# Two queues for the weights of a two-layer streaming encoder: bf16 loads on SyncE, casts paced by matmuls, activation sums moved in the down stage

## The reference

```
layer 0: x += conv_mixers(rmsnorm(x))      # in-projection 1024 -> 2560, two causal convolutions, out-projection
         x += swiglu(rmsnorm(x))           # (silu(h @ Wg) * (h @ Wu)) @ Wd, hidden width 2816
layer 1: x += attention and spatial gating # in-projection 1024 -> 2560, band of 576 keys, out-projection
         x += swiglu(rmsnorm(x))           # other weights
```

## Time and profile before

| | us |
|---|---|
| median of 3 runs | 2945.32 |
| profiled execution | 2949.8 |
| its span (core 0, the slowest) | 2948.3 |
| span of the fastest core | 2926.0 |
| TensorE (PE) busy on core 0 | 2734.8 |
| DVE busy | 1906.9 |
| ACT busy | 1344.7 |
| POOL busy | 472.7 |

### The profile page before, as it was taken

How to read it: one execution, slowest core, us unless ns; L and a number is a source line. 1 busy time by engine, 2 the same in 40 slices (tenths; PEclk the granted TensorE clock), 3 DMA queues, 4 the chain that set the end, 5 groups by cost and what they waited for, 6 DMA issues and landing times.

```text
span 2948.3 us, 49213 instructions; the slowest of 8 cores (2926.0 to 2948.3 us)
## 1 busy us (share of the span) xinstructions
PE 2734.8 (93%) x19840; PEld 1786.7 (61%) x19840; DVE 1906.9 (65%) x3375; ACT 1344.7 (46%) x2538; POOL 472.7 (16%) x946
## 2 busy tenths in 40 slices
PE   6789999767999995999989899999899999999999
PEld 3445555445777773667744555555567777776776
DVE  7667777644555572666757677777665555766655
ACT  2222222133444442555545676677644444454444
POOL 3112211120000011110132344443400000100000
PEclk9889999888999997999999999999999999999999
DMA  9697665796423479784682344445542322534332
GB/s 191 164 177 166 176 171 131 162 142 109 123 78 87 135 193 127 163 190 118 171 166 60 84 111 109 111 114 151 175 138 86 123 78 87 185 129 140 87 129 101
DMA packets 325592, 393.42 MB, mean 133 GB/s; under 512 B 221298, under 2 KB 221826, under 8 KB 325236
## 3 DMA queue, kind: packets, MB, share of 16 engines
q1 hardware_dynamic: 282836, 308.44, 37.6%
q0 software_dynamic: 42528, 81.84, 16.6%
HBM read 255.16 MB, written 167.48 MB: 143 GB/s over the span
## 4 chain that ended last, share of the span: by engine, by line
PE 82%; DMA 6%; DVE 4%; ACT 3%; SPq 3%; POOL 1%; issue 1%; POOLq 0%; DVEq 0%; ACTq 0%
PE ps L687 79%; SPq L717 3%; DMA hT<-h 2%; PE ps L971 2%; DMA xr<-xp 1%; ACT tr L639 1%; DVE xr L650 1%; DMA WiA<-wie 1%; ACT hr L639 1%; DMA WDB<-wdb 1%; PE ps L697 1%; DMA WoC<-woo 1%; DVE hr L654 0%; PE ps L708 0%; POOL E L650 0%
## 5 line engine op out<-in xcount | busy, mean ns | idle before, releaser
L639 ACT ACTIVATE ps<-ps 128x512 f32<-128x512 f32 x720 | 419.6, 583 | 458.8 <-PE ps L687 430.2
L650 DVE TENSOR_TENSOR xr<-ps,xr 128x512 f32<-128x512 f32 (+1 forms) x404 | 272.3, 688 | 162.8 <-PE ps L687 116.0
L687 PE MATMUL ps<-hT,WiA 128*128 128x512 bf16 x1280 | 287.2, 383 | 1.2 <-ACT hT L639 1.1
L639 ACT ACTIVATE hr<-xr 128x1024 bf16<-128x1024 f32 x132 | 138.9, 1052 | 260.3 <-DVE xr L650 196.6
L654 DVE SCALAR_TENSOR_TENSOR hr<-xr,rsr,gain 128x1024 bf16<-128x1024 f32 x132 | 169.2, 1282 | 82.9 <-POOL rsr L650 82.5
L687 PEld LDWEIGHTS ps<-hT,WiA 128*128 128x128 bf16 x1280 | 124.7, 99 | 149.3 <-issue 6.4
L687 PE MATMUL ps<-hT,WGC 128*128 128x256 bf16 x1536 | 187.2, 274 | 9.2 <-DMA WGC<-wgb 5.3
L687 PE MATMUL ps<-hT,WGB 128*128 128x256 bf16 x1280 | 157.5, 275 | 39.3 <-DVE xr L650 33.0
L687 PE MATMUL ps<-hT,WGA 128*128 128x256 bf16 x1536 | 188.0, 275 | 5.8 <-DMA hT<-h 3.7
L687 PE MATMUL ps<-hT,WiC 128*128 128x512 bf16 x768 | 180.4, 379 | 0.7 <-DVE tr L1435 0.4
L687 PEld LDWEIGHTS ps<-hT,WGC 128*128 128x128 bf16 x1536 | 145.2, 98 | 35.3 <-DMA WGC<-wgb 5.9
(11 more groups left out here) (321 smaller groups left out, 5263.4 us busy)
## 6 DMA issues: line engine op xcount, KB each, us to landing
x<-xr SPq DMA_DIRECT2D x160, 512.0 KB, 3.7
xr<-x SPq DMA_DIRECT2D x160, 512.0 KB, 5.7
xr<-xp SPq DMA_DIRECT2D x64, 512.0 KB, 5.8
h<-hr SPq DMA_DIRECT2D x124, 256.0 KB, 3.1
wgb<-wgu POOLq DMA_DIRECT2D x76, 256.0 KB, 14.9
yp<-xr SPq DMA_DIRECT2D x32, 512.0 KB, 3.1
wdb<-wd POOLq DMA_DIRECT2D x44, 256.0 KB, 11.7
WGC<-wgb POOLq DMA_DIRECT2D x12, 512.0 KB, 6.7
```

What stands on the lines that cost most here:

```text
L639: return tag(e.activation(out=R(out), in_=R(in_), func=func, **kw))
L650: return P.add(eng, lambda e, tag: tag(e.tensor_tensor(out=R(out), in0=R(a), in1=R(b), op=op)), [a, b], [out], c)
L687: ins = e.matmul(R(out), l, r, start=st, stop=sp_, skip_group_check=True)
```

## The change

1. Loads from bf16 scratch go to SP's queue, in a stream "wl" of depth 10. Casts stay on POOL's queue in the stream "w", whose depth goes from 6 to 24.
2. `background` takes the place of `cast_some`. Each cast gets a dependence on the matmul that was recorded last before it, so that POOL waits for PE's semaphore (m_pe) ahead of it. The casts are recorded in the hooks behind single gate/up products (in stage A behind its steps), 5 per tile of pass A, 7 of pass B, 5 of stage C, and none behind the last product of a tile.
3. `hsums` gets a dependence on `P.mid`, the matmul that ends the first part of the down stage's second half. `tsums` get a lower priority.
4. The planner's rates change (SP 150 to 230 GB/s, POOL 250 to 200, SP latency 4.0 to 2.5 us), a rule adds a `prime` matmul where no free PSUM bank has been written in full (5 in the program where there were 2), and the down weights of a pass are recorded in its first tile, behind that tile's transposes.

```diff
-        P.depths = {"w": 6, "xl": 6, "xst": 6, "hst": 4, "htr": 4, "ms": 4, "mg": 2, "out": 4}
+        P.depths = {"w": 24, "wl": 10, "xl": 6, "xst": 6, "hst": 4, "htr": 4, "ms": 4, "mg": 2, "out": 4}
-        rate = {"sp": 150e3, "pool": 250e3}
+        rate = {"sp": 230e3, "pool": 200e3}
...
-                op = dma("pool", dst[:, c:c + step], src[:, c:c + step], "w", list(rd), [dst[:, c:c + step]],
-                         step * 128 * (2 if bf else 4))
+                op = dma("sp" if bf else "pool", dst[:, c:c + step], src[:, c:c + step], "wl" if bf else "w", list(rd),
+                         [dst[:, c:c + step]], step * 128 * (2 if bf else 4))
...
-                tt("dve", f(d), f(a), f(b), ALU.subtract, fast=True)
+                tt("dve", f(d), f(a), f(b), ALU.subtract, fast=True, boost=-60)
...
-        def cast_some(ly, p, n):
-            for key in casts[ly, p][:n]:
...
+        def background(n=1):
+            for key in back[:n]:
+                pace = [P.last["pe"]]
...
+                for d in pace:
+                    op.deps.setdefault(d, False)
+            del back[:n]
...
+        def hsums(layer, p, after=None):
+            n0 = len(P.ops)
+            hsums_(layer, p)
+            if after is not None:
+                for op in P.ops[n0:]:
+                    op.deps.setdefault(after, False)
...
             prod(b11, u, 2, (1, 0), order, False)
+            P.mid = P.last["pe"]
...
-            hk = {n: (lambda: cast_some(0, 1, 1)) for n in range(1, 6)} if 0 < t < NT - 1 else {}
+            hk = bg(1, 1, 1, 1, 1)
...
-            hk = {n: (lambda: cast_some(1, 0, 2)) for n in range(0, 5)} if t < NT - 1 else {}
+            hk = {0: lambda: loadC(3)} if lt else bg(2, 2, 2, 1)
```

More of the change, by code:

```diff
@@ L49, in __init__ @@
         self.const = set()
+        self.last = {}
         self.mem = {}
@@ L210, in add @@
         op.deps.pop(op, None)
+        self.last[eng] = op
         self.ops.append(op)
@@ L271, in schedule @@
             best = None
+            if lowa < len(ops) and ops[lowa].nun == 0 and any(p.seed for p in ops[lowa].alloc):
+                fr = [b for b in range(8) if not bank_busy[b]]
+                if fr and not any(bank_full[b] for b in fr):
+                    b = min(fr, key=lambda b: bank_free[b])
+                    op = self.prime(b)
+                    for d in bank_last[b]:
+                        op.deps[d] = False
+                    op.start = max(free["pe"], bank_free[b])
+                    op.end = free["pe"] = op.start + op.cost
+                    bank_free[b], bank_last[b], bank_full[b] = op.end + LAT, [op], True
+                    order["pe"].append(op)
+                    commit.append(op)
             for e in ENG:
@@ L332, in schedule @@
                 srv[e] = s0 + op.nbytes / rate[e]
-                op.end = srv[e] + 4.0
+                op.end = srv[e] + (2.5 if e == "sp" else 4.0)
                 fin = op.end
@@ L1213, in ffn_units, with ffn_tile @@
             return [lambda n=n: gu(n) for n in range(nk)] + [lambda: down(layer, p, t, ring, order)]
-        def ffn_tile(layer, p, t, order, hooks={}, after=()):
+        def ffn_tile(layer, p, t, order, hooks={}, loads=()):
             hload(1 + 2 * layer, t, hT0)
-            hsums(layer, p)
+            hsums(layer, p, P.mid if (layer, p, t) != (0, 0, 0) else None)
+            for f in loads:
+                f()
             for u_ in ffn_units(layer, p, t, UR[2 * layer], order, hooks):
                 u_()
-            for f in after:
-                f()
         def ffn_sample(layer, p, order):
@@ L1232, in ffn_sample @@
                 pt = PT()
+                pt.full = rows == 128
                 mms = []
@@ L1254, in ffn_sample @@
             pt = PT()
+            pt.full = True
             def hl(k, j):
@@ L1280, in loadC @@
             wload(WiC[:, g, :, :].rearrange("p a b -> p (a b)"), I["wio"][:, g, :])
+        back += cast_list(0, range(6), 3)
         for t in range(NT):
@@ L1290, in build_program @@
                       "conv": lambda: [wg_load(0, 0, k, False) for k in (3, 4)], "b": lambda: wg_load(0, 0, 5, False)}
+            elif t >= 2:
+                hk = {x: (lambda n=n: background(n)) for x, n in (("a", 2), ("z", 1), ("conv", 1), ("b", 1))}
             A_tile(t, t + 1 if t + 1 < NT else None, [] if t == 0 else [NT, 3] if t == 1 else [t + 2] if t + 2 < NT else [], hk)
@@ L1296, in build_program @@
         hload(1, NT, hTs)
-        for k in range(6):
-            wd_load(0, 0, k, False)
+        back += cast_list(0, range(6, 11))
+        bg = lambda *ns: {n: (lambda m=m: background(m)) for n, m in enumerate(ns)}
         ld(G[0][:, :], bcast(I["gains"][2:3, :], D))
@@ L1306, in build_program @@
                       5: lambda: wg_load(0, 1, 3, False)}
-            ffn_tile(0, 0, t, order, hk)
+            ffn_tile(0, 0, t, order, hk, [lambda k=k: wd_load(0, 0, k, False) for k in range(6)] if t == 0 else [])
             if t == 0:
                 ffn_sample(0, 0, order)
-        wg_load(0, 1, 4, False)
-        for k in range(5):
-            wd_load(0, 1, k, False)
+        back += cast_list(1, range(6)) + [("c", g, c) for g in range(3) for c in range(4)]
         for t in range(NT):
@@ L1315, in build_program @@
             order = [4, 3, 0, 1, 2] if lt else [0, 1, 2, 3, 4]
-            hk = {n: (lambda: cast_some(1, 0, 2)) for n in range(0, 5)} if t < NT - 1 else {}
[L1317 to L1321, removed]
+            hk = {0: lambda: loadC(3)} if lt else bg(2, 2, 2, 1)
+            ffn_tile(0, 1, t, order, hk, [lambda: wg_load(0, 1, 4, False)] + [lambda k=k: wd_load(0, 1, k, False) for k in range(5)] if t == 0 else [])
             if t == 0:
                 ffn_sample(0, 1, order)
+        background(99)
         loadC(4)
@@ L1570, in build_program, with with_cast, f_ @@
                 fills = smp_[2] + fills
+            if t == 1:
+                back += cast_list(1, range(6, 11))
             if 0 < t < NT - 1:
-                fills = [f_ for u_ in fills for f_ in (u_,)]
-                fills.insert(len(fills) // 2, lambda: cast_some(1, 1, 5))
+                def with_cast(u_):
+                    def f_():
+                        u_()
+                        background(1)
+                    return f_
+                for k in range(5):
+                    n_ = 6 + 4 * k
+                    fills[n_] = with_cast(fills[n_])
             s0 = [u_ for c in range(4) for u_ in C_att(t, qb_, c, 0)]
@@ L1610, in build_program @@
             ffn_tile(1, 0, t, order, hk)
-        for k in range(5):
-            wd_load(1, 1, k, False)
         for t in range(NT):
-            ffn_tile(1, 1, t, list(range(5)))
+            ffn_tile(1, 1, t, list(range(5)), {}, [lambda k=k: wd_load(1, 1, k, False) for k in range(5)] if t == 0 else [])
             if t == 0:
```

29 lines of the change are left out of this document (14 added, 15 removed).

## The result

The changed kernel took 2833.57 (the profiled execution), 2842.51 and 3011.73 us, 2842.51 at the median, against 2945.32 before. The ratio of the other two to before is 0.9637, 95% interval 0.9598 to 0.9677. The forecast was 2852 us.

What follows compares the result with a forecast made beforehand. PE was taken as the bound (busy 2734.8 of 2948.3 us), with stalls from late hT. −43 − 47 − 2 − 9.5 + 6 + 3 + 1 + 0 = −91.5 gave 2858.3, 2853.8 against the median, forecast 2852; range 2816 to 2893.

Steps and rivals of the forecast that it cites:

- What bounds the kernel: First tiles of passes A and B: casts and transposes slow each other, late hT stalls PE, 40.2 and 33.0 us.
- The signs: If right: no PE wait above 15 us behind 600 us, transposes 5 to 11 us, step behind pass A's first tile near 60.
- Paced casts, pass A: End of pass A's first tile: pacing casts lets transposes take 5 to 6 us, a gain of 43 us.
- Pass B: End of pass B's first tile: 47 us gained, and 2.0 at one later step, with 7 casts per tile for 10.
- casts still meet transposes: Rival: each of 16 tiles with casts pays 2.0 us, 32 more, 2884 us; chance 0.13.
- Late sums: Down stage: six xr adds pass ahead of the first sum if hT is late; taken as 0, at worst 85 us.
- Loads on SP: Pass A's start: eight loads (4 MB) ahead of the first transposes, weight sums at lower priority; a gain of 9.5 us.
- The +6 at the other three passes' starts: Starts of passes B, C and D: loads reordered on SP cost 6 us in all, bounds −5 and +20.
- SP's ring: Rival: loads ahead of transposes at four pass starts delay them, 2888 us, at full size 2924; chance 0.07.
- The start: Kernel start: depth 24 puts more casts beside the first tiles' frames, 3 us lost, and three more prime matmuls about 1.
- POOL held by PE: Rival: casts waiting for late matmuls hold POOL's norms, 54 × 2.6 = 140 us, 2992 us; chance 0.05.
- the last rival: Pass A and B starts: transposes slow for another reason, both stalls stay, 2942 us, no change; chance 0.05.

Runs made afterwards that it cites:

- e1: The changed kernel with the casts' dependence on matmuls taken out; ratio to the kernel before 0.9928.
- e6: The kernel before with one edit, the sums of activations depending on the down stage's middle matmul, casts not paced; 2962.45 us.
- e5: The kernel before with one edit: each cast recorded by cast_some depends on the last matmul recorded ahead of it; 2923.09 us.
- e3: The changed kernel with the sums of activations free to run once hT has landed; ratio to the kernel before 0.9624.
- e9: The changed kernel with 12 WiA casts waiting for the fourth norm, pass B's casts 3, 2, 2, sums free, WoC casts later; ratio to the kernel before 0.9620.
- e12: The changed kernel with only 12 WiA casts waiting for the fourth norm and the sums of activations free; 2853.07 and 2854.26 us, 0.965 of the kernel before.
- e8: The changed kernel with the sums of weights at normal priority; 2850.00 us.
- e2: The changed kernel with the bf16 loads back on POOL's queue; 2840.59 and 2848.93 us.
- e4: The changed kernel with the cast stream's depth 6 in place of 24; ratio to the kernel before 0.9655.
- e11: The changed kernel itself, unedited, run once more; 2850.06 to 2860.12 us in five executions, ratio to the kernel before 0.9644.
- e7: The changed kernel with pass A's five paced casts per tile all behind the last gate/up product, at the next transposes; 2843.65 us.

## Why the prediction was right, step by step

*What bounds the kernel.* Right: both long waits for "DVE xr" were hT landing late. e1 and e6 bring back or keep the late hT, and the stall is there whatever stands behind the sum. The signs came too: behind 600 us PE's longest wait is 13.3 us, the transposes of passes A and B take 5.29 to 11.09 us on core 2, and A1 is 61.9.

*Paced casts, pass A.* Forecast −43, measured −41.7 (A1). e5 shows that this one edit does it, e1 that nothing else of the change does.

*Pass B.* Forecast −47 for B1 and −2 for a later step; measured −41.0 and +4.2 for B2 to B5. The mechanism holds (casts away from the transposes), but it was put down to pacing. e5 has pacing with B1 at 73.3, e1 has none with 57.5, so in pass B pacing is neither enough nor needed. What counts is how many casts are in flight at the transposes; how much of that comes from the 7 casts per tile, the last product without casts and the planner's rates is not shown. "A single cast may still be in flight" is right in pass A. In three tiles of pass B it is wrong, four or five are: the transposes at 1133.17, 1180.38 and 1227.80 take 8.61, 9.12 and 11.09 us. So the rival "casts still meet transposes" is true in small. It costs 4.2 us net there, not 32. The "few casts near" of its model tile, the one at 1294.78 before, are seven in flight.

*Late sums.* Forecast 0; e3 finds nothing lost without them, and 3.7 us won in B1 (53.1 there, 53.2 in e9 and 53.3 in e12, against 56.0 to 57.5 in the changed kernel and the others that keep late sums at its rates). So this part of the change costs a little. The prediction's remark that the adds would help if hT is late all the same fails: e6's stall is not shorter than before.

*Loads on SP.* The forecast gain of 9.5 at the first FFN step is 14.3 (A0), half of it from the weight sums' priority (e8), as the prediction put it. The feared cost of eight loads ahead of the transposes isn't seen: those transposes take 10.03 us, and e2 without the loads on SP has the same A0, 59.9. The +6 at the other three passes' starts is −5.1 (B0, and the first two steps of C and D on the mean core). SP's ring as a bound falls.

*The start.* Forecast +4; between −8.6 and +2.3 in two profiles, so not resolved. The step as told was half right: the fourth norm does wait behind 18 casts in POOL's row, and PE with it (22.3 us), but the 14 us wait at 72 us, within the 34.7 of the earlier trace rows, is gone in exchange, and 10.5 are left for xn. That is the depth's doing: with depth 6 both waits go back towards where they were, and the sum of the start stays (e4).

*Stage C.* Taken as 0. L is 7.3 shorter after, 6.7 shorter in e5 with pacing alone, and 6.2 longer in e1 without it. I hadn't counted it. Most of the gain is one step, the third: 86.3 before and 79.7 after, 79.3 in e5, but 79.6 in e1 too, so in the changed kernel it doesn't hang on pacing. The next four steps are 2 to 3 us longer each in e1 (71.8 to 72.3) than after (69.1 to 69.5); that is what pacing saves there. Casts still meet transposes at the start of stage C: POOL issues ten DMAs, half of them WoC's, within the 20.51 us of the first tile's transposes, and PE waits 13.3 us for hT.

*POOL held by PE.* POOL does wait for PE ahead of casts in the changed kernel, 613.7 us in all (411.0 for wgb, 163.0 for wdb, 39.7 for WiC), but PE's waits for xn and E there are 10.5 and 5.5 us, so the rival's price isn't paid; e9 makes one such case in stage C, and PE's wait of 17.0 us follows; how much of it is the held row and how much the WoC casts' meeting the next transposes (17.7 us on the mean core) stays open. So the rival's mechanism may exist; the change doesn't meet its condition, an awaited matmul that lies late.

*The rule on transposes.* The transposes' own time is 5.30 us in the changed kernel and 60.49 in e1, where only the casts' dependence differs. So the last rival, that they are slow there for another reason, is out for pass A. The Trainium skill's "DMA: Bandwidth & Descriptors", under "Rules for kernel authors", has a transpose next to ordinary DMAs need nothing. That row is about transposing streams that corrupt each other's data and says nothing of time; the prediction read it as a rule on time, and as such this trace is against it. Under "Issuing engines are not separate DMA queues" the same page has DMAs of all issuing engines run on the same DMA engines and interleave. This case agrees: casts on POOL's queue slow transposes on SP's (60.49 us in e1), and with the casts paced it makes no difference to the stalls whether the loads are on SP's or POOL's queue (A1 is 61.9 in both, e2). How casts and transposes get in each other's way within the DMA engines is not shown by any run.

The forecast lands 9.5 us above the measured median, and 14.0 above the mean of the two executions in the ratio. The terms that were too small, A0 by 4.8, the pass starts by 11, stage C by 7 and the start by 12.6 (1.7 by e11's profile), outweigh those that were too large, B1 by 6 and the later steps of B by 6. That the total comes so near is luck in part, since these cancel; the largest terms, A1 and B1, which are most of the gain, were right in kind and within 6 us.

## What to carry to other kernels

When an engine idles at the head of its row for a transfer, look at what the DMA engines carry at that time before changing the order behind it: making the row more patient only moved the stall. A background transfer without a wait of its own runs when its queue is free, not when a planner meant it to; tie it to the work that it should run beside, a few at a time, and count how many are still in flight when the transfers on the path start. Five casts beside them cost half a microsecond here, behind a slack that hid the rest; 30 in a row cost 40.

## What was not expected

Four transposes take 5.3 us with no cast or one in flight, 9 to 12 with five just behind them (e7, mean core), 19.18 with ten issued around them within 23 us (e5), 48.66 with 30 in a row at depth 6, and 60.49 with 39 at depth 24 (e1). Not all of a row are in flight at the transposes: counted from issue to landing it is 5 in e7 (14.66 us on the core shown), 8 in e5, 21 before and 34 in e1. That is 1.6 to 2.1 us more for each cast in flight (an estimate: what is over 5.3, divided by the count), and 0.5 to 2.6 over the other tiles of passes A and B with four or more. So the delay grows roughly in step with the casts. In the stalls SP issues nothing else in that time, so residual rows wait as well. PE's wait of 22.3 us in place of 5 at 18 us into the span doesn't show in the sum of the start, since the wait of 14 us further on went away; e4 trades the one for the other and has the same sum.
